# A hybrid decoder layer on one Trainium2 core: the first weight block loaded ahead of x, and routing, one-hot batches, gathers and roundings placed at other blocks of the expert stage

## What is computed

```python
xn = rmsnorm(h, norm1_g)
proj = xn @ w_in                       # 2048 x 5656: retention, sparse attention, gates
ret = retention_group(...)             # 8 heads, decay masks, group norm, silu gate
nsa = nsa_group(...)                   # compressed + selected + window attention, T5 bias
h = h + concat(ret, nsa) @ w_out
h = h + peer_ffn(rmsnorm(h, norm2_g), peer_wq, peer_subkeys, peer_u, peer_v)
out = rmsnorm(h, norm_f_g)

def peer_ffn(x, ...):                  # 8 heads, 16 of 128 x 128 = 16384 experts per head
    s = einsum(q, subkeys); top 16 of each side; top 16 of the 256 sums; gate = softmax
    hid = gelu(einsum('cd,chkd->chk', xc, u[ec]))
    return einsum('chk,chkd->cd', gc * hid, v[ec])
```

## Time and profile before

| | |
|---|---|
| median of three runs | 1953.37 us (1952.35 to 1954.43) |
| profiled execution | 1953.59 us |
| its span, first to last instruction | 1951.8 us |
| PE busy | 1905.3 us, 98% of the span |
| DVE busy | 1208.5 us, 62% |
| ACT busy | 640.9 us, 33% |
| mean granted clock of TensorE | 0.99 |
| DMA | 538.48 MB, mean 276 GB/s |

### The profile page before, as it was taken

The page is one execution under the profiler, slowest core; times in us unless marked ns, Lnnn a source line. Parts: engine busy times, 40 slices in busy tenths (PEclk is TensorE's granted clock), DMA queues, the critical chain, the costliest instruction groups (busy, mean ns, idle before and its releaser), DMA issues.

```text
span 1951.8 us, 29345 instructions
## 1 busy us (share of the span) xinstructions
PE 1905.3 (98%) x11574; PEld 1718.7 (88%) x11574; DVE 1208.5 (62%) x1909; ACT 640.9 (33%) x912; POOL 224.9 (12%) x148
## 2 busy tenths in 40 slices
PE   8999999998999999999989999999999999999998
PEld 7978999898999999899967777789999998777775
DVE  5424666565538389677548888854333334888885
ACT  5213444554432010211135545430000003555554
POOL 0000000000000011121211222212221120021300
PEclk9999999999999999999999999999999999999999
DMA  6665443355453688799988898979999898998884
GB/s 238 209 227 186 142 147 134 146 178 203 160 176 114 209 325 334 267 349 342 367 333 298 314 355 327 344 279 422 361 334 368 341 357 316 351 331 341 331 307 169
DMA packets 79197, 538.48 MB, mean 276 GB/s; under 512 B 8651, under 2 KB 11979, under 8 KB 18060
## 3 DMA queue, kind: packets, MB, share of 16 engines
q1 hardware_dynamic: 57068, 386.33, 53.8%
q0 software_dynamic: 22048, 151.07, 20.3%
HBM read 516.85 MB, written 20.45 MB: 275 GB/s over the span
## 4 chain that ended last, share of the span: by engine, by line
PE 95%; ACT 2%; DVE 1%; DMA 1%; issue 0%; SPq 0%; DVEq 0%; ACTq 0%
PE bank L824 33%; PE bank L540 8%; PE bank L541 7%; PE bank L542 7%; PE bank L913 6%; PE bank L918 6%; PE bank L912 6%; PE bank L919 6%; PE bank L917 6%; PE bank L878 2%; PE bank L629 1%; DMA gate_matrix<-gs 1%; PE bank L838 0%; DVE wmt L1279 0%; PE bank L680 0%; PE bank L699 0%
## 5 line engine op out<-in xcount | busy, mean ns | idle before, releaser
L824 PE MATMUL bank<-hT,raw 128*128 128x192 f32 x4096 | 670.7, 326 | 1.3 <-ACT kept L1225 1.3
L824 PEld LDWEIGHTS bank<-hT,raw 128*128 128x128 f32 x4096 | 665.0, 190 | 2.0 <-issue 2.0
L1658 DVE TENSOR_TENSOR lo<-raw,hi 128x1024 fp32r<-128x1024 f32 x256 | 308.3, 1222 | 106.3 <-ACT hi L1215 106.3
L540 PE MATMUL bank<-act,hi 128*128 128x256 f32 x1216 | 354.2, 291 | 10.8 <-DVE act L1254 6.9
L1215 ACT ACTIVATE hi<-raw 128x1024 fp32r<-128x1024 f32 x256 | 270.6, 1061 | 278.4 <-PE bank L919 278.4
L541 PE MATMUL bank<-act,hi 128*128 128x256 f32 x1216 | 347.1, 285 | 0.0
L542 PE MATMUL bank<-act,lo 128*128 128x256 f32 x1216 | 347.0, 285 | 0.0
L1246 DVE TENSOR_TENSOR lo<-raw,hi 128x2048 fp32r<-128x2048 f32 x76 | 174.1, 2291 | 146.1 <-ACT hi L978 83.9
L540 PEld LDWEIGHTS bank<-act,hi 128*128 128x128 f32 x1216 | 236.5, 194 | 19.9 <-issue 17.8
L1150 ACT ACTIVATE arena<-bank 128x192 f32<-128x192 f32 x128 | 42.4, 331 | 628.3 <-PE bank L824 628.3
L541 PEld LDWEIGHTS bank<-act,hi 128*128 128x128 f32 x1216 | 236.7, 195 | 1.6 <-issue 1.4
...
## 6 DMA issues: line engine op xcount, KB each, us to landing
raw<-in_u SPq DMA_DIRECT2D x128, 1024.0 KB, 6.4
raw<-in_v SPq DMA_DIRECT2D x128, 1024.0 KB, 7.2
raw<-in_w_in SPq DMA_DIRECT2D x44, 1024.0 KB, 5.3
raw<-in_w_out SPq DMA_DIRECT2D x16, 1024.0 KB, 5.2
raw<-in_wq SPq DMA_DIRECT2D x16, 1024.0 KB, 4.9
gate_matrix<-gs POOLq DMA_DIRECT2D x12, 1024.0 KB, 7.1
...
raw<-in_cmp_w SPq DMA_DIRECT2D x8, 1024.0 KB, 4.8
```

The costliest lines, as they stand in the source:

```text
L540: mm(dst, wh, mh, start=first, stop=False)
L824: last = mm(bank[s % 2][:, 0:TD], raw[:, s, k * P:(k + 1) * P], xn[:, k, 0:TD], start=(k == 0), stop=(k == KT - 1))
L1658: vec.tensor_tensor(lo[:, mv % 2, cols], raw[:, mv % RAW, cols], hi[:, mv % 2, cols].bitcast(F32), ALU.subtract).then_inc(v_lo_ready, 1)
```

## The change

At the start, SP issues the first weight block first, then gains and x in four pieces; ACT issues the bias and one-hot tables, loads the table set with both Ln and Exp, issues `base` and the gate weights, and rounds block 0 before x. DVE forms block 0's remainder before those of x. PE begins with the small bias matmuls; block 0 waits for x piece by piece (`grain=1`). The bias rows become one matmul with 8 rows of output, which POOL stores 128-fold and reads back skewed. The sum of squares is made in four additions over three rounds, its matmul stands behind block 2, and blocks 0 and 1 are evacuated unscaled and multiplied by `rstd` later. A second table load stands ahead of the `w_out` blocks' second half. In the expert stage the numbers `ROUTED`, `EXP_SPARSE`, `EXP_DENSE`, `PAIRS_LISTED`, `FIRST_GATHERS` and `STAGE_ITEMS` change; the first one-hot batch stands one block later in relation to `ROUTED`; and ACT rounds the first v block of each half ahead of the last gelu.

```diff
-ROUTED = 36
+ROUTED = 32
 GATE_BLOCKS, BATCHES = HALF - ROUTED, TD // 8
-EXP_SPARSE, EXP_DENSE, PAIRS_LISTED = 15, 34, 18
-FIRST_GATHERS = 12
+EXP_SPARSE, EXP_DENSE, PAIRS_LISTED = 10, 27, 13
+FIRST_GATHERS = 14
...
-STAGE_ITEMS = ((PAIRS_LISTED, ROUTED, FIRST_GATHERS), (ROUTED, HALF - 2, 22), (HALF, 2 * HALF, 25),
-               (2 * HALF, 3 * HALF, 47), (3 * HALF, 4 * HALF - 10, 22))
+STAGE_ITEMS = ((PAIRS_LISTED, ROUTED, FIRST_GATHERS), (ROUTED, HALF - 4, 24), (HALF, 2 * HALF, 26),
+               (2 * HALF, 3 * HALF - 3, 42), (3 * HALF, 4 * HALF - 10, 22))
```

SP, POOL and PE at the start:

```diff
-            sp.dma_start(rb[0:N_BUCKETS, :], a["rel_bias"]).then_inc(bias_in_loaded, 16)
-            sp.dma_start(onehots[0:N_BUCKETS + 1, :], a["onehots"]).then_inc(bias_in_loaded, 16)
-            sp.dma_start(gains[:, :], a["gains"]).then_inc(gains_loaded, 16)
-            for x in range(2):
-                sp.dma_start(hT[:, x * 2048:(x + 1) * 2048], a["xT"][:, x * 2048:(x + 1) * 2048]).then_inc(x_loaded[x], 16)
...
-            sp.dma_start(base[:, :], a["base"]).then_inc(base_loaded, 16)
             load(a["w_in"][0], 0)
-            sp.dma_start(wg, a["w_gate"]).then_inc(wg_loaded, 16)
+            sp.dma_start(gains[:, :], a["gains"]).then_inc(gains_loaded, 16)
+            for x in range(4):
+                sp.dma_start(hT[:, x * 1024:(x + 1) * 1024], a["xT"][:, x * 1024:(x + 1) * 1024]).then_inc(x_loaded[x], 16)
             for n in range(1, RAW):
                 load(a["w_in"][n], n)
+            load_after(a["w_in"][4], 0, 0)
+
+            load_after(a["w_in"][5], 1, 1)
             sp.wait_ge(act_lo_ready, KT)
             sp.wait_ge(sq_ready, 1)
-            sp.wait_ge(ss_ready, 1)
             sp.dma_start(mid, a["mid"]).then_inc(mid_loaded, 16)
             sp.dma_start(hT[:, 832:1344], a["cmp_w2"]).then_inc(mid_loaded, 16)
...
-            sp.wait_ge(rows_copied, NSA_HEADS)
-            sp.dma_start(rows_dram.rearrange("h p n -> p h n"), bias).then_inc(rows_stored, 16)
-
...
+            pool.wait_ge(rows_copied, 1)
+            pool.dma_start(rows_dram, head_rows.unsqueeze(1).to_broadcast([NSA_HEADS, P, BIAS_W])).then_inc(rows_stored, 16)
+            pool.wait_ge(rows_stored, 16)
+            pool.wait_ge(block_done, PAIRS)
+            for part in range(2):
+                first = P * (1 - part)
+                skew = bass.AP(tensor=rows_dram.tensor, offset=P - 1 + first,
+                               ap=[[BIAS_W - 1, P], [P * BIAS_W, NSA_HEADS], [1, P * (part + 1)]])
+                pool.dma_start(bias[:, :, P * part:P * part + P * (part + 1)], skew).then_inc(bias_loaded, 16)
...
-                    if act_count and k % 4 == 0:
-                        pe.wait_ge(act_hi_ready, act_count + act_step * (k // 4))
-                        pe.wait_ge(act_lo_ready, act_count + act_step * (k // 4))
+                    if act_count and k % grain == 0:
+                        pe.wait_ge(act_hi_ready, act_count + k // grain)
+                        pe.wait_ge(act_lo_ready, act_count + k // grain)
```

```diff
-            def bias_rows(h):
-
-                mm(bank[2 + h % 4][:, 0:BIAS_W], rb_wide[0:rows, h, :], onehots[0:rows, 0:BIAS_W],
-                   start=True, stop=True).then_inc(rows_ready, 1)
-
-            pe.wait_ge(rb_wide_ready, 1)
             pe.wait_ge(bias_in_loaded, 32)
-            for h in range(4):
-                bias_rows(h)
-
-
+            pe.wait_ge(consts_ready, 2)
             for w in range(8 + NCMP):
                 z = BIAS_W + 256 - CMP_STRIDE * (w - 8) - (CMP_LEN - 1)
                 last = mm(bank[6][:, w * 8:w * 8 + 8], onehots[0:rows, z:z + P], rb[0:rows, :], start=True, stop=True)
             last.then_inc(cbias_ready, 1)
-            weights_block(0, 0, act_count=4, act_step=4)
+            weights_block(0, 0, act_count=1, grain=1)
+            mm(bank[2][0:NSA_HEADS, 0:BIAS_W], rb[0:rows, :], onehots[0:rows, 0:BIAS_W], start=True, stop=True).then_inc(rows_ready, 1)
+            weights_block(1, 1)
+            weights_block(2, 2)
 
             pe.wait_ge(base_loaded, 16)
             pe.wait_ge(sq_summed, 1)
-            mm(bank[7][:, 0:T], ones, sq_sum[:, 0:T], start=True, stop=True).then_inc(ss_ready, 1)
-            weights_block(1, 1)
-            weights_block(2, 2)
-            for h in range(4, 8):
-                pe.wait_ge(rows_copied, h - 3)
-                bias_rows(h)
+            mm(bank[7][:, 0:T], ones, sq[:, 0, :], start=True, stop=True).then_inc(ss_ready, 1)
             weights_block(3, 3)
 
```

ACT, the start and the two table loads:

```diff
+            ac.dma_start(rb[0:N_BUCKETS, :], a["rel_bias"]).then_inc(bias_in_loaded, 16)
+            ac.dma_start(onehots[0:N_BUCKETS + 1, :], a["onehots"]).then_inc(bias_in_loaded, 16)
+            nc.scalar.preload_act_table_set("natural_log_exp_and_others")
+            ac.dma_start(base[:, :], a["base"]).then_inc(base_loaded, 16)
+            ac.dma_start(wg, a["w_gate"]).then_inc(wg_loaded, 16)
+            round_static(0)
             ac.wait_ge(gains_loaded, 16)
             for k in range(KT):
-                if k % 8 == 0:
-                    ac.wait_ge(x_loaded[k // 8], 16)
+                if k % 4 == 0:
+                    ac.wait_ge(x_loaded[k // 4], 16)
                 do(act[:, k, 0:T], hT[:, k * T:(k + 1) * T], ACT.Copy, scale=g1[:, k:k + 1]).then_inc(act_hi_ready, 1)
-            round_static(0)
-            do(sq.rearrange("p k t -> p (k t)"), hT[:, :], ACT.Square).then_inc(sq_ready, 1)
-            ac.wait_ge(consts_ready, 1)
             for m in range(1, PAIRS):
                 round_static(m)
                 if m == 1:
-                    for h in range(4):
-                        ac.wait_ge(rows_ready, h + 1)
-                        do(bias[:, h, :], bank[2 + h][:, 0:BIAS_W], ACT.Copy).then_inc(rows_copied, 1)
-                    ac.wait_ge(ss_ready, 1)
-                    rsqrt(bank[7][:, 0:T], rstd[:, :], D, log_ready, rstd_ready, 1)
+                    do(sq.rearrange("p k t -> p (k t)"), hT[:, :], ACT.Square).then_inc(sq_ready, 1)
                 if m == 2:
+                    ac.wait_ge(rows_ready, 1)
+                    ac.wait_ge(act_lo_ready, KT)
+                    ac.wait_ge(sq_ready, 1)
+                    do(head_rows, bank[2][0:NSA_HEADS, 0:BIAS_W], ACT.Copy).then_inc(rows_copied, 1)
                     ac.wait_ge(wg_loaded, 16)
                     do(wg_r[:, :, 0:24], wg, ACT.Copy).then_inc(wg_hi_ready, 1)
                 if m == 3:
-                    for h in range(4, 8):
-                        ac.wait_ge(rows_ready, h + 1)
-                        do(bias[:, h, :], bank[2 + h % 4][:, 0:BIAS_W], ACT.Copy).then_inc(rows_copied, 1)
+                    ac.wait_ge(consts_ready, 2)
+                    ac.wait_ge(ss_ready, 1)
+                    rsqrt(bank[7][:, 0:T], rstd[:, :], D, log_ready, rstd_ready, 1)
...
+            nc.scalar.preload_act_table_set("natural_log_exp_and_others")
             for c in range(9):
                 round_static(M_OUT2 + c)
```

DVE, the start:

```diff
-            dv.wait_ge(bias_in_loaded, 32)
-            dv.wait_ge(consts_ready, 2)
-            vec.tensor_copy(rb_wide[0:N_BUCKETS + 1, :, :],
-                            rb[0:N_BUCKETS + 1, :].unsqueeze(2).to_broadcast([N_BUCKETS + 1, 8, P])).then_inc(rb_wide_ready, 1)
+            rest_static(0)
             dv.wait_ge(gains_loaded, 16)
             for k in range(KT):
-                if k % 8 == 0:
-                    dv.wait_ge(x_loaded[k // 8], 16)
+                if k % 4 == 0:
+                    dv.wait_ge(x_loaded[k // 4], 16)
                 dv.wait_ge(act_hi_ready, k + 1)
                 vec.scalar_tensor_tensor(out=act[:, k, T:2 * T], in0=hT[:, k * T:(k + 1) * T], scalar=g1[:, k:k + 1],
                                          in1=act[:, k, 0:T].bitcast(F32), op0=ALU.mult, op1=ALU.subtract).then_inc(act_lo_ready, 1)
-            rest_static(0)
+            def unscaled_block(m):
+
+                dv.wait_ge(block_done, m + 1)
+                vec.tensor_copy(tile(m), bank[m % 2][:, 0:T]).then_inc(acc_evacuated, 1)
+
             for m in range(1, PAIRS):
+                if m == 2:
+                    dv.wait_ge(sq_ready, 1)
+                    vec.tensor_tensor(sq[:, 0:8, :], sq[:, 0:8, :], sq[:, 8:16, :], ALU.add).then_inc(sq_step, 1)
+                if m == 3:
+                    for x, half in enumerate((4, 2, 1)):
+                        dv.wait_ge(sq_step, x + 1)
+                        vec.tensor_tensor(sq[:, 0:half, :], sq[:, 0:half, :], sq[:, half:2 * half, :], ALU.add
+                                          ).then_inc(sq_step if half > 1 else sq_summed, 1)
+                    unscaled_block(1)
+                if m == 4:
+                    dv.wait_ge(rstd_ready, 1)
+                    scaled(2, 2, tile(2))
+                    dv.wait_ge(acc_evacuated, 2)
+                    vec.tensor_tensor(tile(0, 2).rearrange("p (f t) -> p f t", f=2), tile(0, 2).rearrange("p (f t) -> p f t", f=2),
```

(25 more changed lines are left out.)

55 lines of the change are left out of this document (26 added, 29 removed).

## The result

The changed kernel takes **1925.39 us** (median of 4 runs, 1924.49 to 1925.96); the kernel before, run beside it, takes 1953.61. The ratio is 0.9856 (95% interval 0.9839 to 0.9873): 28.2 us faster. The forecast was 1921.0, range 1915 to 1930. The profiled execution took 1925.02.

The account below looks back on a forecast made before the run. TensorE was taken as the bound, its waits few and single. Gains of 14.7+1.3+6.4-0.5+6.1+4.4 = 32.4 us took the profiled 1953.59 to 1921.2, or 1921.0 as a median; range 1915 to 1930.

Parts of the forecast that it names:

- a first block after 16: Sign of a wrong forecast: TensorE starting the first weight block later than 16 us into the kernel.
- A: Kernel start: earlier first weight block 5.6, no sum-of-squares wait 4.7, clock behind it 2.3, fewer wide matmuls 2.1; gain 14.7 us.
- rival 2: Start: small matmuls begin late, behind the weight block, at 6.1; 2 us less gain, 1923, at worst 1927; chance 0.11.
- B: Table loads at the second rsqrt: the load between Ln and Exp moves to an existing ScalarE wait; gain 1.3 us.
- C: Expert-stage routing ends four blocks earlier: the 4.65 us wait before the first one-hot batch goes, plus clock; gain 6.4 us.
- The walk: Item-by-item count of VectorE's routing with gathers landing in 9.0 us: ends at 763, 4 us before TensorE's transposes.
- Rivals 1 and 4: Routing gathers land slower: at 11 us each, 1930, chance 0.12; at 16 us, 1961, chance 0.02.
- D: First v block, first half: earlier gate load and rounding cut the wait from 6.2 to 1.6; with clock, gain 6.1 us.
- Rival 3: Wait before the first v block stays because gates, v rows and residual share the DMA: 6.1 us lost, 1927; chance 0.06.
- E: Second half's first v block: rounding moved likewise, wait of 4.4 falls to 1.6; with clock 1.5, gain 4.4 us.
- Rival 5: Start: TensorE's low clock lasts a block longer after the earlier start, 4.3 us lost, 1925; chance 0.03.
- the prediction's "nothing": Bias store and loads moved from SP to POOL land after block 8, are used after block 20: no effect on time.

## Why the prediction was right, and where not

The time lies in the range, 4.4 us above the point, and each edit worked through the mechanism named, but two of the five sizes were too large. Of the prediction's own signs of being wrong one is there, a first block after 16 (16.4), and of its signs of being right two are missing, a first weight matmul near 14 and, at the first v block, 1.6 us of waiting with a clock of 1.00 behind it. By the steps:

- **A, 14.7: mis-sized, 12.0.** The step "I take 4.1, near the first, for the table is a ninth of a block" failed. The table landed at 6.5, above even the upper bound of 6.1: rival 2, with its price of 2 us (2.4 in the trace). (The lower bound was read from a copy that VectorE was said to have ended by 3.6; in the trace the copy, of the bias table, begins at 3.59, when the one-hot table lands. The bound stands.) I had drawn against rival 2 on the Trainium skill (DMA: Bandwidth & Descriptors, "SWDGE vs HWDGE vs iDMA"), which has each DMA engine take its queues in turn, and had taken this to bring a small transfer in early. The table took 5.3 us from its issue beside the weight block, 3.5 with half a megabyte on the other queue, and 2.4 with only its own queue's transfers behind it. In this kernel a small transfer beside a large one waited nearly as long as the large one; so did the 24 KB of gains on SP's own queue behind the block, 5.5 us where before they took 2.0. The table on ScalarE's queue with nothing large beside it was not tried, so a part of that queue in the 5.3 us is not excluded. The rest of A (4.7, 2.3, 2.1, and 5.6 once the table is early) came as sized.
- **B, 1.3: right,** 1.35 between the marks, and 1.3 when undone. The 2.66 of the Trainium skill (ScalarE: Activation LUTs, "What ACT_TABLE_LOAD costs") would be 2.7; the traces speak for their row, the medians leave it open.
- **C, 6.4: right,** 6.5, and the 0.5 for the risk was not needed. The walk gave 4 us to spare, the trace shows 3.2, and the experiment with Exp five blocks later turned that into 25.5 us of delay. Rivals 1 and 4 did not occur: the landings of 7 of the 14 gathered rows of this stretch show in the trace, 5.6 to 10.3 us, 8.1 in the mean. That the walk's end came true within 1 us is in part luck: for landings of 8 us it had 759, 4 us sooner than the 763.8 of the trace, and what it left out is not shown.
- **D, 6.1: mis-sized, 4.3.** Two steps failed. "Lands at about 981": on the new scale some 961.2 (19.8 us earlier), and it landed at 962.6, in another execution at 964.7, because it was issued right behind a v block. And "through, with the remainder, by 982.3" left out that the remainder stands on VectorE behind the multiplication that waits for the gates: with ScalarE done at 960.8, VectorE began it only at 963.1. So the wait was 2.4 instead of 1.6, and the clock, counted as kept, was lost. With the load ahead of the block all of it was there: wait 1.5, clock 1.00. Rival 3 was right about the resource, not about its size.
- **E, 4.4: right,** 4.5: wait 1.4, clock 1.00. Undone, it cost 5.8.
- **Rival 5** occurred in a small part: the low clock lasted 5.2 us into block 0, until 21.7, where before it had lasted 3.9, and 1.3 us more at half the clock cost 0.6.

The sum fell short where the price of a transfer was taken from its size instead of from what else moved at that moment. With both transfers moved, and two loads more out of their way, the kernel ran at 1920.4, where the forecast had put the change.

## What to carry to other kernels

When a load is moved, list what is issued just before and behind it on every queue (here within 0.5 us): its own size says little beside a 1 MB block, and the consumer's in-order queue makes everything behind it late too. For a wait that ends last, look at what comes second (here the rounding, 2 us behind the gate load) before pricing its removal. And start from the trace's row, but for a wait like those of 2.3 us and more here, count the clock behind it too.

## What had not been expected

- **The clock behind short waits.** Of seven executions with a wait of 2.3 to 2.6 us before the first v block, six lost clock (v half 308.8 to 309.5 us) and one did not (307.48, the row at 965.23 above). Behind waits of 1.4 and 1.5 us the half took 307.5 to 308.0, behind 4.4 to 6.0 us 309.6 to 310.4. So a wait of 2.4 us may cost 1.3 to 2.1 us more, or nothing. What ended the wait does not tell them apart: by the list of waits it was ScalarE's rounding in four of the seven, the one without a loss among them, and VectorE's remainders in three.
- **A clock below 1.00 without a wait.** Between 160 and 190 us every profile shows 0.74 to 0.97 in one or two stretches of 10 us with TensorE busy all through; the loss is 1.7 us in nine of the fourteen profiles and 3.4 or 3.5 in five, whatever the kernel. What this makes of the scatter between executions is not shown: in one kernel the profiled execution lost 3.4 there and was the fastest of five (1922.34). In every profile it lies at the same work, 32 matmuls of only 15 columns and the passes behind them. In the changed kernel (timeline of PE):

```profile
164.70 3.64 PE L647 MATMUL bank<-hT,arena 128*128 128x15 f32 x32
```

They are issued 0.11 us apart, with no wait (the last idle time before them, 1.1 us, ends at 158.9), and the passes of 256 columns behind them step at 0.21 us until 171.8; the clock is 0.84 and 0.82 in the two windows of 5 us from 165. Before the change the 32 stand at 176.65 to 180.1, and the clock is 0.66 in the 5 us from 180. That they are the cause was not tried.

- **A slow store.** DMA issues of the changed kernel (KB each, median us from issue to landing):

```profile
gate_matrix<-gs POOLq DMA_DIRECT2D x12, 1024.0 KB, 13.2
...
bias_rows<-hT POOLq DMA_DIRECT2D x1, 1536.0 KB, 36.3
...
rows_sb<-in_u_rows,pairs POOLq DMA_INDIRECT x64, 9.0
```

The bias store, written in another form and issued from POOL, landed 36.3 us after its issue, where that of before had taken 8.2. No engine's wait in the list goes back to it: the prediction's "nothing" held. The gate stores, of the same size as before, took 13.2 us in the median instead of 7.1. This belongs to the expert stage's part of the change: the median is 7.0 in the kernel with the start alone and 13.5 in the one with the expert stage alone. In POOL's order each of the last stores now stands about 1 us behind an indirect gather (934.33, store 935.26), where before it stood ahead of one (store 941.66, gather 943.18); whether that is the cause was not tried. The last store is issued at 935.3 and lands at 951.5, so of the 18 us until the gate load is issued at 953.8 it sets 16; the rest is SP's order, in which v block 1 comes first, at 953.4.
